# Eight sample rows ride along as extra columns of the last token tile, and the S5 state products alternate between the two column halves of the array

## The chip, the cores and the metric

The kernel runs on one core of a Trainium2 chip, as one program. The metric is the device time of an execution in microseconds (us), the median of several. Five engines work side by side: TensorE (PE), whose matmuls stream a moving operand past stationary weights, VectorE (DVE), ScalarE (ACT), GpSimd (POOL), and SyncE (SP), which here only issues transfers. Each takes its instructions in order and waits for semaphores that the others raise.

## The reference

One layer of a hybrid model is computed in fp32, for a prompt of 2048 tokens and for 8 sample rows (one new token of each of 8 sequences, with a carried S5 state):

```python
proj = x @ w_in                                   # 1024 -> 1536
u = gelu(proj[..., :512])
v = layer_norm(gelu(proj[..., 512:1024]), ln_v_g, ln_v_b)
xs = proj[..., 1024:]                             # 32 groups of 16
y_a = u * chunk_spatial_gate(v, w_s, b_s)         # chunks of 128 tokens; a sample row is a chunk of 1
y_b, h_re, h_im = s5_mixer(xs, h0, ...)           # a complex state of 64 numbers for each group
mix = concatenate([y_a, y_b]) @ w_out
x = layer_norm(ALPHA * x + mix, ln1_g, ln1_b)
x = layer_norm(ALPHA * x + grouped_moe(x, ...), ln2_g, ln2_b)
```

The outputs are the new rows of prompt and sample, the last S5 states of both, and the sample's normalised v.

## The kernel before

The work goes through stages, each a block of five engine programs with a barrier behind it. The change touches the first three.

**Precision.** Most products use operands split into a high and a low part (F32R), three matmuls for one: high x high, high x low, low x high (`PARTS`). The products of S5 are plain fp32, and one of these matmuls runs as two passes of weight load and matmul.

**Projection stage (to about 256 us).** Tokens go in 8 halves of 256 (`NH = 8`, `XH = 256`). PE transposes rows (`turn`, L690), ACT rounds them to the high part (`high`, L408), DVE takes the low part (`low`, L483); both parts lie in `xt[high/low][:, i % 2]`. `one(i, f, w)` (matmuls L702) forms 128 output channels x 256 tokens, 24 matmuls, for xs (`w = 0`, banks `pxs`, evicted by DVE at L496) and for u (`w = 1`, banks `pu`, evicted with the GELU by ACT at L420). From half 4 on PE also forms S5's matrices for one pair of groups after each tile (`pair_mats`, L720 and L729) from what DVE computes (`v_pair`, L637 to L640; `results`, L647, L649), while POOL computes another table (L377 to L380). ACT and DVE also split pieces of w_down, which SP loads and stores (L302, L295). In the last half the four xs tiles come first, with a `pair_mats` behind each, and then the four u tiles. Then ACT, DVE and POOL split the weights of v (L468, L674, L397), while PE runs 26 dummy matmuls, 52 passes (L789).

The 8 sample rows are transposed after the first half (`xts`, 8 columns for each k). Ahead of half 4 PE multiplies them on their own, with the sample as the stationary operand and 512 channels streamed past:

```python
for w, banks, out in ((0, pxs, xs_out), (1, pu, u_out)):
    pe.wait_ge(out, i * FT)
    for k in range(KD):
        for x, h in PARTS:
            mm = t.matmul(banks[0][0:NS, :], xts[x][:, k, :], (w_hi, w_lo)[h][w][:, k, :], ...)
    mm.then_inc(us_prod, 1)
pe.wait_ge(us_out, 2)
```

ACT (L455) and DVE (L654) evict the two results to `us[8, 2, 512]`, and SP stores the xs part (L313).

**Gate stage (to about 379 us).** PE forms v for 16 token tiles from the turned rows (L1138, `half` reloads them, L880), ACT applies the GELU, DVE normalises, PE multiplies by the chunk matrix (`gate`, L1116), DVE and POOL (L951, the last four tiles) multiply into u. The sample's v is one block of 24 matmuls (L1127), its gating is in `sample()` on DVE. SP spreads the stored xs of the sample into `us1`, with eight transfers of 4-byte pieces (L894).

**S5 stage (to about 470 us, then its gate).** There are 16 pairs of groups in quads of four. PE's order is `states(p + 1)`, `outputs(p)`, and so on, and after each quad 16 transposes (L1482) that wait for ACT (L1284, L1291). `states` multiplies 128 x 128 inputs by matrices for 64 state rows: group g = 0 goes to array columns 0 to 63, g = 1 to 64 to 127, with two accumulating 128-column matmuls (L1450) and one 8-column matmul for the sample (L1451) each, for the real and for the imaginary part. DVE scans (L1344 to L1366), and `outputs` has a part that needs no scan (L1461, L1462) and one that does (L1469). `load` (L815 to L817) brings a pair's inputs as soon as the outputs four pairs before are done. DVE's waits and the semaphores set the order; nothing is planned at run time.

Of the kernel before, what the change touches and what calls it, by code (L numbers as in the profile page):

```python
# [6 lines left out]
P = 128  # L7
F32 = mybir.dt.float32
# [7 lines left out]
ALU = mybir.AluOpType  # L16
# [81 lines left out]
def hybrid_step(nc, a, o):  # L98
    ctx = ExitStack()
    with ctx, nc.allow_non_contiguous_dma(reason="small parameters are laid out by state"):  # L100
# [28 lines left out]
        us_dram = dram("u_sample", [NS, WA])  # L129
# [5 lines left out]
        xt_dram = [dram(f"x_turned_{n}", [NH, P, KD * XH]) for n in ("high", "low")]  # L135
# [22 lines left out]
        xts = [sb(f"xts_{n}", [P, KD, NS], F32R) for n in ("high", "low")]  # L158
# [4 lines left out]
        us = sb("us", [NS, 2, WA])  # L163

# [8 lines left out]
        xt = [sb(f"xt_{n}", [P, 2, KD, XH], F32R, where=pa) for n in ("high", "low")]  # L173
        wv_raw = sb("w_v", [P, KD, WA], where=Place(nc, base))
        wv = [sb("wv_high", [P, KD, WA], F32R, where=Place(nc, base + 96 * KB)), sb("wv_low", [P, KD, WA], F32R, where=Place(nc, base))]
        pb = Place(nc, base + 96 * KB)
        xin = sb("xin", [P, 4, D], where=pb)
        xin_r = sb("xin_r", [P, 4, D], F32R, where=Place(nc, base + 96 * KB))
# [19 lines left out]
        with phase() as ph:  # L198
# [8 lines left out]
             dch, ach, gch, xsT_prod, xsT_out, k_stored, d_masked, kz, us_prod, us_out, cb_zero, k_zeroed, prm_row, prm_turned,  # L207
# [3 lines left out]
             cq_ready ust_ready dch ach gch xsT_prod xsT_out k_stored d_masked kz us_prod us_out cb_zero k_zeroed prm_row  # L211
# [42 lines left out]
            def _(sp):  # L254
# [51 lines left out]
                for i in range(NH):  # L306
                    if i < NH - 2:
                        sp.wait_ge(x_lo_set, 4 * i + 4)
                        for n in range(2):
                            sp.dma_start(xt_dram[n][i], xt[n][:, i % 2].bitcast(F32).rearrange("p k n -> p (k n)")).then_inc(xt_stored[i % 2], 16)  # L310
# [89 lines left out]
            def _(act):  # L400
                def high(c):
# [5 lines left out]
                    for h in range(2):  # L407
                        nc.scalar.copy(xt[0][:, i % 2, 4 * h:4 * h + 4, c % 2 * P:(c % 2 + 1) * P],  # L408
# [2348 lines left out]
```

## Time and profile before

| | us |
|---|---|
| median of 3 runs (lowest, highest) | 1299.25 (1299.21, 1302.53) |
| profiled execution, its own time | 1302.82 |
| its span in the trace | 1301.2 |
| PE busy in the span | 1213.3 (93%) |
| DVE, ACT, POOL busy | 901.8, 533.4, 483.9 |
| mean granted clock of PE | 0.972 |

The time of an execution is 1.6 us above its span. Busy time of PE counts overlapping matmuls as one stretch, and a matmul's end is modelled, so that start times tell more than durations. A granted clock of 1.00 is 2.4 GHz, and 0.50 is 1.2 GHz; a value between is a stretch with both.

### The profile page before, as it was taken

Reading aid. Unit: us, or ns where it says so; the run is one execution under the profiler, and the core shown is the slowest. Engines: PE = TensorE matmul, PEld = TensorE weight load, DVE = VectorE, ACT = ScalarE, POOL = GpSimd, SP = SyncE. Lnnn points to the kernel's source line nnn. Section 1 sums busy time; section 2 is a strip of 40 time slices with the busy share of each in tenths; the row PEclk is TensorE's granted clock in tenths of the full one; section 3 lists DMA queues with packets and bytes.
Section 4 is the critical chain, followed back from the end, with each engine's and each line's share of the span. In section 5 each row is a group of like instructions: output and inputs, shape, how many; then the busy total and the mean of one; then the engine's idle time right before and its main releaser. Section 6 shows DMA issues by size and latency. Waiting matters only on the chain. (4 is left out here: it accounts for less than half of the span.)

```text
span 1301.2 us, 24203 instructions
## 1 busy us (share of the span) xinstructions
PE 1213.3 (93%) x7245; PEld 1011.6 (78%) x7246; DVE 901.8 (69%) x1917; ACT 533.4 (41%) x881; POOL 483.9 (37%) x584
## 2 busy tenths in 40 slices
PE   7999999999878888999999688999999999999976
PEld 7997999978767755788887587888888888887852
DVE  3464886558868656557678567777787777777767
ACT  4131111111002346122333125666666666666656
POOL 3007880100031110623232033545555555455446
PEclk9999999999979989999999879999999999999988
DMA  8689593584436764246679565989889879756496
GB/s 246 192 316 290 181 267 123 170 265 167 160 106 211 216 223 120 100 155 240 236 265 300 200 259 210 293 266 322 262 270 327 257 230 294 196 155 169 107 296 254
DMA packets 141303, 290.08 MB, mean 223 GB/s; under 512 B 54634, under 2 KB 71610, under 8 KB 129940
## 3 DMA queue, kind: packets, MB, share of 16 engines
q1 hardware_dynamic: 122868, 225.70, 49.9%
q0 software_dynamic: 17328, 61.41, 19.2%
q10 hardware_dynamic: 1040, 2.10, 0.4%
q8 instruction: 39, 0.64, 0.2%
q14 instruction: 28, 0.23, 0.1%
HBM read 177.90 MB, written 111.13 MB: 222 GB/s over the span
## 5 line engine op out<-in xcount | busy, mean ns | idle before, releaser
L2407 DVE TENSOR_TENSOR wgu<-w_raw,wgu (+1 forms) x192 | 229.9, 1220 | 89.0 <-ACT wgu L2510 88.7
L2673 PE MATMUL p_gu<-wgu,xg_high 128*128 x768 | 244.4, 399 | 9.2 <-issue 4.6
L2510 ACT CAST wgu<-w_raw x188 | 192.7, 1052 | 62.2 <-issue 62.0
L2673 PEld LDWEIGHTS p_gu<-wgu,xg_high 128*128 128x128 f32 x768 | 139.7, 189 | 43.7 <-issue 17.3
L2673 PE MATMUL p_gu<-wgu,xg_low 128*128 x384 | 150.7, 392 | 0.0
L2272 POOL TENSOR_TENSOR spare_e<-nothing 128x1 f32<-128x1 f32 x48 | 46.5, 969 | 217.2 <-DVE yo L2426 217.2
L2273 POOL DMA_INDIRECT acc_rows<-yo,si x48 | 112.3, 2339 | 8.7 <-issue 8.5
L1995 PE MATMUL p_out<-w_out_high,mixt_high 128*128 128x512 f32 x256 | 102.3, 400 | 0.0
L1995 PE MATMUL p_out<-w_out_low,mixt_high 128*128 128x512 f32 x256 | 100.6, 393 | 0.0
L1995 PE MATMUL p_out<-w_out_high,mixt_low 128*128 128x512 f32 x256 | 100.6, 393 | 0.0
L2673 PEld LDWEIGHTS p_gu<-wgu,xg_low 128*128 128x128 f32 x384 | 72.1, 188 | 15.5
L2697 PE MATMUL p_d<-wd_high,ht_high 128*128 x192 | 80.2, 418 | 1.3 <-DVE ht_low L2420 1.3
L420 ACT ACTIVATE ya<-pu 128x256 f32<-128x256 f32 x32 | 12.2, 383 | 167.0 <-PE pu L702 167.0
L702 PE MATMUL pxs<-xt_high,w_xs_high 128*128 128x256 f32 x256 | 76.3, 298 | 2.7 <-DVE xt_low L483 2.0
L2697 PE MATMUL p_d<-wd_high,ht_low 128*128 x192 | 75.9, 395 | 0.0
L2697 PE MATMUL p_d<-wd_low,ht_high 128*128 x192 | 75.7, 394 | 0.0
L702 PE MATMUL pxs<-xt_high,w_xs_low 128*128 128x256 f32 x256 | 74.0, 289 | 0.0
L702 PE MATMUL pxs<-xt_low,w_xs_high 128*128 128x256 f32 x256 | 73.9, 289 | 0.0
L2400 DVE TENSOR_TENSOR xg_low<-p_xt,xg_high 128x512 fp32r<-128x512 f32 x96 | 61.8, 685 | 16.3 <-ACT xg_high L2497 16.1
L702 PE MATMUL pu<-xt_high,w_u_high 128*128 128x256 f32 x256 | 72.6, 284 | 0.0
L702 PE MATMUL pu<-xt_high,w_u_low 128*128 128x256 f32 x256 | 72.5, 283 | 0.0
L702 PE MATMUL pu<-xt_low,w_u_high 128*128 128x256 f32 x256 | 72.5, 283 | 0.0
(521 smaller groups left out, 2951.0 us busy)
## 6 DMA issues: line engine op xcount, KB each, us to landing
w_raw<-in_w_gate SPq DMA_DIRECT2D x16, 1024.0 KB, 7.3
w_raw<-in_w_up SPq DMA_DIRECT2D x16, 1024.0 KB, 9.9
wd_high<-w_down_high SPq DMA_DIRECT2D x16, 1024.0 KB, 6.7
wd_low<-w_down_low SPq DMA_DIRECT2D x16, 1024.0 KB, 9.0
ya_u<-in_w_down SPq DMA_DIRECT2D x38, 256.0 KB, 4.8
w_down_low<-ya_r SPq DMA_DIRECT2D x38, 256.0 KB, 5.7
acc_rows<-ax SPq DMA_DIRECT2D x18, 512.0 KB, 6.8
xin<-in_x_prompt SPq DMA_DIRECT2D x16, 512.0 KB, 5.3
```

The lines of the kernel that those rows point to most:

```text
L420: nc.scalar.activation(ya[:, 2 * i:2 * i + 2, f, :], pu[f % 2][:, 0:XH].rearrange("p (t n) -> p t n", n=P), ACT.Gelu_apprx_tanh).then_inc( ...
L702: mm = t.matmul(banks[f % 2][:, 0:XH], (w_hi, w_lo)[h][w][:, k, f * P:(f + 1) * P], xt[x][:, i % 2, k, :], start=(k == 0 and x + h == 0), ...
L1995: mm = t.matmul(po[b][m][0:n, :], mixt[x][:, b, k, 0:n], wo[w][:, k, m * SUP:(m + 1) * SUP], start=(k == 0 and x + w == 0), stop=(k == KD ...
L2272: gp.tensor_tensor(spare[:], nothing[:], nothing[:], ALU.add)
L2273: gp.indirect_dma_start(acc_dram, bass.IndirectOffsetOnAxis(ap=si[:, b:b + 1], axis=0), yo[:, b, :], None, compute_op=ALU.add).then_inc(ad ...
L2400: low = tt(xl[:, b, part, :], pt_x[h], xh[:, b, part, :].bitcast(F32), ALU.subtract)
L2407: low = tt(wgu[:, slot, 1, at], raw[:, slot, at], wgu[:, slot, 0, at].bitcast(F32), ALU.subtract)
L2510: nc.scalar.copy(wgu[:, slot, 0, at], raw[:, slot, at]).then_inc(hi_set, 1)
L2673: mm = t.matmul(pg[b][:, :, :], x[:, b, k, :], w[h][:, k], start=(k == 0 and x is xh and h == 0), stop=(k == KD - 1 and x is xl))
L2697: mm = t.matmul(pd[m][:, :], ht[x][:, b, k, :], w[h][:, k, m * SUP:(m + 1) * SUP], start=(k == 0 and x + h == 0), stop=(k == 1 and x == 1))
```

## The change

The sample rows become columns 256 to 263 of the odd buffer of turned rows, and the last half (7, odd) is projected 264 columns wide. Their results come out as [channel, sample] and are evicted by small extra instructions. In the gate stage the sample's u is multiplied after a transpose, and its xs is transposed back with four matmuls. In S5 the loops over h (which of the two accumulating matmuls) and g (which column half) are swapped, so that successive matmuls go to different halves.

```diff
-        xts = [sb(f"xts_{n}", [P, KD, NS], F32R) for n in ("high", "low")]
+        us_t = sb("us_t", [P, 2, FT, NS], where=Place(nc, us_at))
-        xt = [sb(f"xt_{n}", [P, 2, KD, XH], F32R, where=pa) for n in ("high", "low")]
+        XC = [XH, XH + NS]
+        xt = [[sb(f"xt_{n}{i}", [P, KD, XC[i]], F32R, where=pa) for i in range(2)] for n in ("high", "low")]
+        xts = [xt[n][1][:, :, XH:] for n in range(2)]
 # SP, projection
+                        if i % 2:
+                            sp.wait_ge(xsT_lo, 1)
-                    if i == NH // 2:
-                        sp.wait_ge(us_out, 2)
-                        sp.dma_start(us_dram, us[:, 1, :]).then_inc(k_stored, 16)
...
+                sp.wait_ge(xs_smp, FT)
+                sp.dma_start(us_dram.rearrange("(f p) n -> p f n", p=P), us_t[:, 1]).then_inc(k_stored, 16)
 # ACT, u_tile
+                    if i == NH - 1:
+                        nc.scalar.activation(us_t[:, 0, f, :], pu[f % 2][:, XH:XH + NS], ACT.Gelu_apprx_tanh).then_inc(u_smp, 1)
 # DVE, xs_tile
+                    if i == NH - 1:
+                        v.tensor_copy(us_t[:, 1, f, :], pxs[f % 2][:, XH:XH + NS]).then_inc(xs_smp, 1)
 # PE, one
+                    cols = XH + NS if i == NH - 1 else XH
+                    if i == NH - 1:
+                        pe.wait_ge(xsT_lo, 1)
+                        if f >= 2:
+                            pe.wait_ge((xs_smp, u_smp)[w], f - 1)
-                            mm = t.matmul(banks[f % 2][:, 0:XH], ..., xt[x][:, i % 2, k, :], ...)
+                            mm = t.matmul(banks[f % 2][:, 0:cols], ..., xt[x][i % 2][:, k, 0:cols], ...)
 # PE, ahead of half 4: the block of 48 matmuls quoted above, its waits and both evictions are gone
 # SP, gate stage
-                for n in range(NS):
-                    sp.dma_start(us1[P - Q:P, :, n], us_dram[n].rearrange("(g q) -> q g", q=Q)).then_inc(us_in, 16)
+                sp.dma_start(us1[P - Q:P], us_dram.rearrange("(g q) n -> q g n", q=Q)).then_inc(us_in, 16)
 # DVE, sample(): the 8x512 product is gone; at the end of the stage
-                v.tensor_copy(mixs_t[:, 0:FT, :], pmt[:, :].rearrange("p (f s) -> p f s", s=NS)).then_inc(mixa_set, 1)
+                v.tensor_tensor(mixs_t[:, 0:FT, :], pmt[:, :].rearrange("p (f s) -> p f s", s=NS), us_t[:, 0], ALU.mult).then_inc(mixa_set, 1)
+                v.tensor_copy(us[:, 1, :], psv[:, :]).then_inc(mixa_set, 1)
 # PE, after the last v tile
+                        for f in range(FT):
+                            mm = t.transpose(psv[:, f * P:(f + 1) * P], us_t[:, 1, f, :], ident[:])
 # PE, states
                     for r in range(2):
+                        lhs = [[smat[:, slot, h, r, g * N:(g + 1) * N] for h in range(2)] for g in range(2)]
+                        dst = [pst[b][g * N:(g + 1) * N, r, :] for g in range(2)]
+                        for h in range(2):
+                            for g in range(2):
+                                t.matmul(dst[g][:, 0:K], lhs[g][h], umat[:, slot, h, g, 0:K], start=(h == 0), stop=(h == 1))
                         for g in range(2):
-                            lhs = [smat[:, slot, h, r, g * N:(g + 1) * N] for h in range(2)]
-                            dst = pst[b][g * N:(g + 1) * N, r, :]
-                            for h in range(2):
-                                t.matmul(dst[:, 0:K], lhs[h], umat[:, slot, h, g, 0:K], start=(h == 0), stop=(h == 1))
-                            mm = t.matmul(dst[:, K:K + NS], lhs[1], umat[:, slot, 1, g, K:K + NS], start=True, stop=True)
+                            mm = t.matmul(dst[g][:, K:K + NS], lhs[g][1], umat[:, slot, 1, g, K:K + NS], start=True, stop=True)
```

Buffers behind the turned rows move by 512 bytes or 1 KB, and the stored turned rows get room for 264 columns a row block. These moves change no instruction count.

## Rows read from the trace of the kernel before

**Rows 1.** The windows of five stretches: busy us and instructions of each engine, clock, DMA.
```profile
114.80:126.80 12.00, 11.33 (x50) 4.19 (x49) 4.55 (x9) 0.97 (x2) 10.04 (x14) 1.00 0.94 268
159.00:164.00 5.00, 5.00 (x31) 5.00 (x31) 4.96 (x9) 0.00 (x0) 4.75 (x7) 0.66 0.69 218
256.50:367.00 110.50, 107.08 (x511) 87.03 (x512) 84.76 (x332) 11.42 (x20) 9.89 (x20) 0.98 0.53 180
371.00:386.00 15.00, 9.85 (x70) 9.51 (x71) 6.73 (x25) 0.00 (x0) 10.04 (x11) 0.54 0.54 158
390.00:470.00 80.00, 68.03 (x622) 55.47 (x618) 58.95 (x241) 28.66 (x54) 11.82 (x22) 1.00 0.63 198
```

**Rows 2.** The timeline of PE around the sample's block: start us, us, what.
```profile
114.74 0.28 PE L702 MATMUL pu<-xt_low,w_u_high 128*128 128x256 f32 x1
114.86 0.40 PE L772 MATMUL pxs<-w_xs_high,xts_high 128*8 128x512 f32 x1
...
126.81 0.39 PE L702 MATMUL pxs<-xt_high,w_xs_high 128*128 128x256 f32 x1 [0.67 <-ACT us L455]
```

**Rows 3.** The timeline of PE, first and last of one tile's 24 matmuls.
```profile
129.79 0.28 PE L702 MATMUL pu<-xt_high,w_u_high 128*128 128x256 f32 x1
...
132.55 0.28 PE L702 MATMUL pu<-xt_low,w_u_high 128*128 128x256 f32 x1
```

**Rows 4.** SP's timeline there, and the issues' view: KB, us to landing.
```profile
118.98 1.33 SPq L302 DMA_DIRECT2D ya_u<-in_w_down  x1
...
126.78 0.29 SPq L313 DMA_DIRECT2D u_sample<-us  x1
136.27 0.35 SPq L323 DMA_DIRECT2D sq_mats<-s_mat  x1
...
ya_u<-in_w_down SPq DMA_DIRECT2D x11, 256.0 KB, 5.1
```

**Rows 5.** The timeline in the last half, DVE and PE's weight loads.
```profile
233.65 0.22 DVE L649 COPY k_lag<-pkv 128x64 f32<-128x64 f32 x1
...
235.59 0.42 DVE L640 TENSOR_TENSOR v_im<-tv 128x256 f32<-128x256 f32 x1
236.31 0.14 PEld L720 LDWEIGHTS pst<-ident,v_re 128*128 128x128 f32 x1
...
237.06 0.68 DVE L647 COPY s_mat<-pst 128x512 f32<-128x512 f32 x1
...
238.94 0.07 DVE L671 MEMSET tm<- 128x16 f32 x1
```

**Rows 6.** The timeline at the end of the projection stage.
```profile
243.08 2.52 SPq L331 DMA_DIRECT2D k_lags<-k_lag  x2
...
247.78 5.35 DVE L674 TENSOR_TENSOR wv_low<-w_v,wv_high 128x512 fp32r<-128x512 f32 x4 [0.35 <-ACT wv_high L468]
...
249.26 5.96 PE L789 MATMUL tp<-ident 128*128 128x128 f32 x52
```

**Rows 7.** SP's timeline early in the gate stage.
```profile
258.20 1.35 SPq L887 DMA_DIRECT2D g_col<-in_ln_v_g  x1
```

**Rows 8.** The timeline at the end of the gate stage.
```profile
377.47 0.18 DVE L1105 COPY mixs_t<-pmt 128x32 f32<-128x32 f32 x1
...
377.64 1.26 POOL L951 TENSOR_TENSOR ya<-k_lag,ya 128x512 f32<-128x512 f32 x1 [0.44 <-DVE k_lag L1048]
```

**Rows 9.** The timeline of PE in two state products, at the low and full clock.
```profile
380.78 0.22 PE L1451 MATMUL p_state<-umat,sq 128*64 128x8 f32 x1
380.84 0.42 PE L1450 MATMUL p_state<-umat,sq 128*64 128x128 f32 x1
380.85 0.25 PE L1451 MATMUL p_state<-umat,sq 128*64 128x8 f32 x1
...
381.27 0.33 PE L1451 MATMUL p_state<-umat,sq 128*64 128x8 f32 x2
...
427.44 0.68 PE L1450 MATMUL p_state<-umat,sq 128*64 128x128 f32 x6
427.90 0.23 PE L1451 MATMUL p_state<-umat,sq 128*64 128x8 f32 x2
...
428.72 0.23 PE L1451 MATMUL p_state<-umat,sq 128*64 128x8 f32 x2
```

**Rows 10.** The waits of 380 to 470 us: total us, times, longest.
```profile
DVE rot L1344 <- PE p_state L1451: 10.9, 4, 3.2
```

**Rows 11.** The timeline of S5, DVE's hst and PE's outputs, and PE's wait.
```profile
399.41 0.28 DVE L1362 TENSOR_TENSOR hst<-rot 128x128 f32<-128x128 f32 x1
...
400.01 1.14 PE L1469 MATMUL p_y<-sq,hst 64*128 64x256 f32 x8
...
419.01 0.71 PE L1450 MATMUL p_state<-umat,sq 128*64 128x128 f32 x6 [1.47 <-DMA sq<-sq_mats]
```

More of the change, by code:

```diff
@@ L134, in hybrid_step @@
         NH = SEQ // XH
-        xt_dram = [dram(f"x_turned_{n}", [NH, P, KD * XH]) for n in ("high", "low")]
+        xt_dram = [dram(f"x_turned_{n}", [NH, P, KD * (XH + NS)]) for n in ("high", "low")]
         x1_dram = dram("x1_rows", [SEQ + NS, D])
@@ L407, in high @@
                     for h in range(2):
-                        nc.scalar.copy(xt[0][:, i % 2, 4 * h:4 * h + 4, c % 2 * P:(c % 2 + 1) * P],
+                        nc.scalar.copy(xt[0][i % 2][:, 4 * h:4 * h + 4, c % 2 * P:(c % 2 + 1) * P],
                                        tp[h][:, :].rearrange("p (k n) -> p k n", k=4)).then_inc(x_hi_set, 1)
@@ L443, in _ @@
                 act.wait_ge(xsT_prod, 1)
-                nc.scalar.copy(xts[0][:], tp[0][:, 0:KD * NS].rearrange("p (k n) -> p k n", n=NS)).then_inc(xsT_out, 1)
+                nc.scalar.copy(xts[0], tp[0][:, 0:KD * NS].rearrange("p (k n) -> p k n", n=NS)).then_inc(xsT_out, 1)
                 for f in range(FT):
@@ L452, in _ @@
                 for i in range(2, NH - 1):
-                    if i == NH // 2:
-                        act.wait_ge(us_prod, 2)
-                        nc.scalar.activation(us[:, 0, :], pu[0][0:NS, :], ACT.Gelu_apprx_tanh).then_inc(us_out, 1)
                     for f in range(FT):
@@ L480, in low @@
                     for h in range(2):
-                        part = (slice(None), i % 2, slice(4 * h, 4 * h + 4), slice(c % 2 * P, (c % 2 + 1) * P))
+                        part = (slice(None), slice(4 * h, 4 * h + 4), slice(c % 2 * P, (c % 2 + 1) * P))
                         dve.wait_ge(x_hi_set, 2 * c + h + 1)
-                        v.tensor_tensor(xt[1][part], tp[h][:, :].rearrange("p (k n) -> p k n", k=4),
-                                        xt[0][part].bitcast(F32), ALU.subtract).then_inc(x_lo_set, 1)
+                        v.tensor_tensor(xt[1][i % 2][part], tp[h][:, :].rearrange("p (k n) -> p k n", k=4),
+                                        xt[0][i % 2][part].bitcast(F32), ALU.subtract).then_inc(x_lo_set, 1)
                 def w_low(f):
@@ L699, in one @@
                         pe.wait_ge(out, n - 1)
+                    cols = XH + NS if i == NH - 1 else XH
[3 more added lines that the diff above has]
+                            pe.wait_ge((xs_smp, u_smp)[w], f - 1)
                     for k in range(KD):
                         for x, h in PARTS:
-                            mm = t.matmul(banks[f % 2][:, 0:XH], (w_hi, w_lo)[h][w][:, k, f * P:(f + 1) * P],
-                                          xt[x][:, i % 2, k, :], start=(k == 0 and x + h == 0), stop=(k == KD - 1 and x == 1))
+                            mm = t.matmul(banks[f % 2][:, 0:cols], (w_hi, w_lo)[h][w][:, k, f * P:(f + 1) * P],
+                                          xt[x][i % 2][:, k, 0:cols], start=(k == 0 and x + h == 0), stop=(k == KD - 1 and x == 1))
                     mm.then_inc(prod, 1)
@@ L766, in _ @@
                         pe.wait_ge(c_copied, 2)
-                        pe.wait_ge(xsT_lo, 1)
-                        for w, banks, out in ((0, pxs, xs_out), (1, pu, u_out)):
-                            pe.wait_ge(out, i * FT)
-                            for k in range(KD):
-                                for x, h in PARTS:
-                                    mm = t.matmul(banks[0][0:NS, :], xts[x][:, k, :], (w_hi, w_lo)[h][w][:, k, :],
-                                                  start=(k == 0 and x + h == 0), stop=(k == KD - 1 and x == 1))
-                            mm.then_inc(us_prod, 1)
-                        pe.wait_ge(us_out, 2)
                     for f in range(FT):
@@ L819, in hybrid_step @@
         with phase() as ph:
-            pt = Place(nc, base + 128 * KB)
+            pt = Place(nc, base + 129 * KB)
             wst = sb("wst", [P, HA, P], where=pt)
```

43 lines of the change are left out of this document (21 added, 22 removed).

## The prediction

> **What bounds the kernel now.** I read the windows by stage first [rows 1]. TensorE (PE) is busy for 11.33 of the 12.00 us around the sample's projection, and for 68.03 of the 80 us in the middle of the S5 stage. So time taken from PE is worth something where PE is the last to be ready, and nothing where it waits. Which of the two holds is read from the timeline, stage by stage. The change touches three stages: the input projection (to about 256 us), the spatial gate (to 379 us) and S5 (to about 470 us). Everything behind them (output projection, experts, last norm) keeps its instructions, and each of those stages starts behind a barrier, so it only moves.
>
> In the timeline of PE [rows 2] the reader should look at start times, not at durations. The ordinary matmuls before the sample start 0.12 us apart; the last one starts at 114.74. Then come the 48 matmuls of L772, and the first ordinary one afterwards starts at 126.81. The stretch is 11.95 us from 114.86 to 126.81, and there PE does nothing but the sample: 8 stationary columns with 512 streamed past, plus a last wait of 0.67 us for the GELU on ScalarE. In the steady run 24 such ordinary matmuls span 2.76 us from the first start to the last, 0.120 us each [rows 3].
>
> **Part 1, the sample leaves its own block.** Gone are the 48 matmuls, both waits for the evictions, the two evictions and PE's wait for them. Were the stretch cut out, the next matmul would start at 114.86. That is 11.95 us, all of it on PE. Is PE the last one there? VectorE (DVE) works 4.55 us of the 12, ScalarE (ACT) 0.97 [rows 1]. POOL is busy for 10.04 us, but with tables for S5 whose stores are due much later. So I take the full 11.95 us.
>
> What could be late next is SyncE's queue (SP). It issued a load of w_down at 118.98, whose kind lands 5.1 us after issue, and it then stood idle until the sample's result at 126.78, with the next transfer at 136.27 [rows 4]. After the change the first projection of the next half ends near 120.6, and ACT then wants to round that w_down piece, which is there only near 125.4 (118.98 + 1.33 + 5.1). ACT stands for about 4.5 us, and behind it in its queue is the rounding of the next turned rows. These are wanted by PE only at the next turn two projections later, some 14 us on, so I cost it at nothing. If that cover is gone it costs up to 4.5 us.
>
> **Part 2, 264 columns in the last half.** The last of the eight 256-row halves has 8 output tiles x 24 = 192 matmuls, each 8 columns wider. The trace has no width of 264. From below: nothing, if the start distance of 0.120 us is set by the weight load beside it. From above: in proportion to the columns, 0.120 x 8/256 = 3.75 ns, times 192 = 0.72 us. I take the middle, 0.35 us, since both are small. The Trainium skill (TensorE: Matmul & The Clock Gate, section Back-to-back issue gap) puts the distance at N/2.4 + 2.5 ns, 109 ns for 256 columns and 112.5 for 264. The measured 120 ns is above both; by the rule the sum would get 0.64 us here in place of 0.35.
>
> The small evictions: DVE copies 128x8 ahead of each of four xs tiles, ACT does a 128x8 GELU ahead of each of four u tiles. I bound one by a memset of 128x16, 0.07 us, and a copy of 128x64, 0.22 us [rows 5]. In the last half the loop PE -> DVE -> PE is close: DVE ends the second product of a pair at 236.01, PE starts to turn it at 236.31 [rows 5]. So there is 0.3 us of cover per tile against 0.07 to 0.22: nothing; without the cover 4 x 0.22 = 0.9 us. ACT's four are done while PE still spins: PE's dummy products run from 249.26 to 255.22, DVE is done at 253.13, ACT before that [rows 6].
>
> The store of the sample's xs goes from the middle to the end, as 512 pieces of 32 B, in SP's queue ahead of the two stores of k_lag. Its issue takes 0.29 us as the old one did [rows 4], or at most 1.35 us like the 512-piece load of g_col [rows 7]. The k_lag stores were issued by 245.6, and PE holds the barrier until 255.2 [rows 6]. Nothing. The odd halves of the turned rows are stored and reloaded 256 B per partition longer; no matmul of the gate stage waits for them, PE is busy for 107.08 of 110.50 us there [rows 1]. Nothing again.
>
> **Part 3, the gate stage.** One load instead of eight for the sample, of 32 B pieces instead of 4 B: SP's queue is some 3 us earlier, but nobody waits for it. Four extra transposes on PE stand ahead of the gates of the last tiles, which wait for DVE and POOL. At the end DVE multiplies 128x32 instead of copying it, and copies 8x512 more (0.18 us before [rows 8]; with the 0.68 us of a 128x512 copy [rows 5] it is 0.86, to 378.33), while POOL multiplies until 378.90 [rows 8]. Cover left: 0.5 us. DVE also loses one 8x512 product in the middle, where PE bounds. Nothing in all.
>
> **Part 4, S5's state products.** For a pair of groups PE runs 24 passes on a 64-column half each (an fp32 matmul is two passes). In the trace the first six 128-column passes start before the first 8-column pass [rows 9], although in program order the fourth is followed by two 8-column passes of the same half. And in the slow-clock stretch a 128-column pass (380.84) starts between two 8-column passes [rows 9]. So the chip already lets the other half overtake, once the first half's fourth weight load is out. From the first start 427.44 the 8-column passes start at 427.90 and then on to 428.72, 0.273 us for each of three more groups. Two groups, 0.55 us, are the time of one half; the second half merely starts one group late. Alternating should let it start at once: 0.27 us less a pair. With the clock low the same offset is 0.49 us, from 380.78 to 381.27 [rows 9]. From below the gain is nothing (the overlap is there already); from above all 16 pairs at 0.27 plus 0.2 us more at the low clock, 4.5 us.
>
> Where does it reach the end? The waits [rows 10] say that DVE waited 4 times for a state product, 10.9 us in all: at the first pair and at each quad's start, after the transposes. There a shorter product counts in full.
> - First pair, clock low [rows 9]: 0.5 us.
> - Rest of the first quad: the scans catch up. DVE ends hst at 399.69, the outputs start at 400.01 [rows 11]. Only 0.3 us can be gained.
> - Second and third quad: the first product counts (0.27, it also brings forward the load of the quad's last). The next two run into a wait for that load, 1.47 us at 419.01 [rows 11], and gain nothing. The last counts again. 2 x 2 x 0.27 = 1.1 us.
> - Last quad: DVE scans bound it after its first product: 0.27 us.
> Sum 2.2 us. The Trainium skill (TensorEngine Tiling, section Theoretical Speedup) promises up to 2x for a 64-wide operand. By it the products would halve, 1.3 to 0.65 us; the trace says that most of this is had already.
>
> **Sum.** -11.95 + 0.35 - 2.2 = -13.8 us. The profiled execution took 1302.82 us (its span 1301.2), 0.3% above the median of the runs, 1299.25; in its own terms it becomes 1289.0. From the median: 1285.5 us.
>
> **Rivals.**
> - *The order in S5 does nothing*, because the second half is held back by something else than the order (the issue of passes). For it: the groups run at an even 0.27 us. Against: with the clock at the lower level the offset grows to 0.49 us, so it is the array and not the issue. Then -11.95 + 0.35 = -11.6: 1287.6 us.
> - *The gap was SP's time to catch up.* The late w_down piece holds ACT 4.5 us and this reaches PE. For it: DMA share 0.94 in the gap [rows 1]. Against: the 14 us of cover above. -9.3: 1289.9 us.
> - *The halves run wholly side by side* (the rule of the second page above): the saving per counted product is 0.65 instead of 0.27, so 5 x 0.65 + 1.0 + 0.3 = 4.6: 1283.0 us.
> - *The clock falls in S5: slower than before.* With less work PE may no longer keep 2.4 GHz. Its granted clock was 1.00 in 390 to 470 at 85% busy, and 0.54 in 371 to 386 at 66% busy, after an idle stretch [rows 1]. At 1.2 GHz its 68 us of work would grow by up to as much again. It decides from about 16 us at the lower level (13.8/0.85); with half the stage it is +34 - 13.8 = +20: 1319 us. Against it: the change takes only 2 to 4 us of PE's 68.
> Beside these, single dips like 159 to 164 (clock 0.66) come or go with any shift, 1.7 us each way; they are part of each case's own range.
>
> **Chances.** Forecast 0.60 (1283 to 1288.5), no gain in S5 0.16, catching up 0.08, halves side by side 0.07, clock falls 0.05, and 0.04 for a gain eaten to within 0.3% by something not seen. A measurement of this kernel can tell about 0.3% from no change, 3.9 us. All cases but the last two lie beyond it: faster 0.91, same 0.04, slower 0.05. The range 1281.5 to 1291 takes in the first four cases with their dips.
>
> **What would show it.** In the new profile: no block of 128*8 matmuls in the projection, and PE's starts 0.12 us apart across the border of the halves; the last half's starts 0.120 to 0.124 apart; the projection's end 11.6 us earlier; the gate stage of the same length; the first and last 8-column passes of a pair's product 0.27 us nearer to the first start than 1.28; S5 shorter by 2.2 us, with the waits of DVE for p_state down by about 1.3. Wrong it would be if ACT or PE wait for DMA near the old gap, or PEclk in S5 drops.

## The result, and the profile after

The changed kernel took 1283.30 us (median of 4 runs, 1282.77 to 1285.56) against 1299.23 us for the kernel before beside it (4 runs): ratio 0.9876, 95% interval 0.9852 to 0.9900. That is 15.9 us less, between 13 and 19 by the interval. The forecast was 13.8 less, 1285.5 us. The profiled execution took 1283.07 us, its span 1281.4.

A comparison of two traces alone would mislead: the spans differ by 19.8 us. Some 3 us of that lie at the expert lists, whose code is the same, where the profiled execution before ran with TensorE (PE) at the lower clock. So I read each stage from its own first and last matmul, and over several kernels. Two kinds of stretch recur below: the projection, from the first turn of input rows to the last u matmul; and the gate stage's v stretch, from the first to the last v tile.

The windows of the kernel after, to be held against [rows 1]: length, busy us and count of PE, its weight loads, DVE, ACT, POOL, then granted clock, DMA share, GB/s.

```profile
114.80:126.80 12.00, 11.61 (x100) 11.37 (x99) 8.98 (x12) 2.36 (x5) 9.97 (x15) 1.00 0.98 315
250.00:360.50 110.50, 105.30 (x520) 85.23 (x519) 84.22 (x318) 12.03 (x21) 11.63 (x20) 1.00 0.49 177
371.00:386.00 15.00, 12.71 (x130) 10.46 (x127) 14.03 (x54) 2.48 (x7) 3.79 (x5) 0.97 0.68 200
390.00:450.00 60.00, 50.48 (x497) 40.96 (x496) 45.97 (x189) 20.87 (x39) 8.61 (x16) 1.00 0.66 204
```

In the first window 12 us hold 100 instructions on PE instead of 50: the block is gone and the ordinary projection stands there. DVE is busy for 8.98 us of it, not 4.55. S5 keeps its clock at 1.00.

PE's timeline at the border of the halves, where L772 stood before [rows 2], and one pair's product in S5, which answers to the full-clock rows of [rows 9]:

```profile
114.64 0.28 PE L709 MATMUL pu<-xt_low,w_u_high 128*128 128x256 f32 x1
114.76 0.28 PE L709 MATMUL pxs<-xt_high,w_xs_high 128*128 128x256 f32 x1
...
392.31 0.66 PE L1451 MATMUL p_state<-umat,sq 128*64 128x128 f32 x8
392.80 0.24 PE L1453 MATMUL p_state<-umat,sq 128*64 128x8 f32 x4
392.89 0.64 PE L1451 MATMUL p_state<-umat,sq 128*64 128x128 f32 x8
393.35 0.24 PE L1453 MATMUL p_state<-umat,sq 128*64 128x8 f32 x4
```

The border is 0.12 us wide. The product now runs as two even parts, and from first to last matmul it takes 1.08 us where it took 1.34 in all the kernels with the old order: 0.26 less, the forecast's 0.27. The first 8-column pass comes no earlier (0.49 us after the first start, 0.46 before [rows 9]); only the end does.

PE's waits in the projection stage (us, times, longest), first of the kernel before, then of the kernel after:

```profile
PE pxs L702 <- DVE xt_low L483: 2.0, 1, 2.0
PE pst L720 <- DVE v_im L640: 2.0, 1, 2.0
```

```profile
PE pst L727 <- DVE v_im L645: 4.3, 5, 1.4
PE pxs L709 <- DVE xt_low L486: 2.0, 1, 2.0
```

PE now waits five times for DVE's v_im, the second operand of the S5 matrices that PE turns between projections. The other traces agree: 3.4 to 4.3 us in three to five waits in the kernels with the change, 1.0 to 2.0 us in one wait in those before (e4 and e8, below, left aside).

PE's waits in the gate stage, before and after, the first of which the prediction had not looked at:

```profile
PE pg L1116 <- DVE ya L1058: 3.4, 1, 3.4
```

```profile
PE pg L1114 <- DVE ya L1057: 2.3, 1, 2.3
```

And what lay ahead of and behind the longer wait, first in the timeline of the kernel before:

```profile
342.98 0.68 DVE L1071 TENSOR_TENSOR mixs<-mixs,us 8x512 f32<-8x512 f32 x1
...
346.17 1.13 PE L1116 MATMUL pg<-wst,vn 128*128 128x128 f32 x8 [3.36 <-DVE ya L1058]
```

The windows behind it:

```profile
347.00:351.00 4.00, 4.00 (x13) 3.16 (x12) 3.19 (x12) 0.00 (x0) 0.55 (x1) 0.57 0.03 6
357.00:361.00 4.00, 4.00 (x21) 3.38 (x20) 3.23 (x12) 0.21 (x1) 0.55 (x1) 1.00 0.00 0
```

The product of the sample rows (L1071) is gone in the changed kernel. PE's wait is 1.1 us shorter, and the stretch with 13 instead of 21 matmuls in 4 us (granted clock 0.57, so mostly the lower of the two levels, 1.2 GHz) is gone too. The v stretch went from 110.17 to 108.19 us. The prediction had costed this edit at nothing.

S5's waits of DVE, the row of [rows 10] after the change; it is 2.2 us less, where the forecast was 1.3:

```profile
DVE rot L1345 <- PE p_state L1453: 8.7, 4, 2.3
```

### The profile page after: what moved, and what is told of

It is laid out like the page before. It is cut to its first block and busy times, and to the rows that moved or that the text cites. A ratio compares the mean times of both kernels' runs of the same rounds, so it can differ in the third digit from the quotient of the medians.

```text
span 1281.4 us, 24124 instructions
## 1 busy us (share of the span) xinstructions
PE 1193.0 (93%) x7201; PEld 997.3 (78%) x7202; DVE 908.0 (71%) x1920; ACT 533.6 (42%) x884; POOL 482.3 (38%) x584
## 3 DMA queue, kind: packets, MB, share of 16 engines
q0 software_dynamic: 17328, 61.41, 19.8%
## 5 line engine op out<-in xcount | busy, mean ns | idle before, releaser
L709 PE MATMUL pxs<-xt_high,w_xs_high 128*128 128x256 f32 (+1 forms) x256 | 75.4, 294 | 2.0 <-DVE xt_low L486 2.0
L709 PE MATMUL pxs<-xt_high,w_xs_low 128*128 128x256 f32 (+1 forms) x256 | 73.1, 286 | 0.0
L709 PE MATMUL pxs<-xt_low,w_xs_high 128*128 128x256 f32 (+1 forms) x256 | 72.9, 285 | 0.0
L1730 POOL TENSOR_TENSOR mixt_low<-ya,mixt_high 128x512 fp32r<-128x512 f32 x16 | 26.6, 1662 | 121.8 <-ACT mixt_high L1800 121.7
L709 PE MATMUL pu<-xt_high,w_u_high 128*128 128x256 f32 (+1 forms) x256 | 72.4, 283 | 0.0
L709 PE MATMUL pu<-xt_high,w_u_low 128*128 128x256 f32 (+1 forms) x256 | 72.2, 282 | 0.0
L709 PE MATMUL pu<-xt_low,w_u_high 128*128 128x256 f32 (+1 forms) x256 | 72.2, 282 | 0.0
```

The costliest lines, as they stand in the source:

```text
L709: mm = t.matmul(banks[f % 2][:, 0:cols], (w_hi, w_lo)[h][w][:, k, f * P:(f + 1) * P], xt[x][i % 2][:, k, 0:cols], start=(k == 0 and x + h ...
L1730: gp.tensor_tensor(mixt[1][:, b, part, 0:n], src, mixt[0][:, b, part, 0:n].bitcast(F32), ALU.subtract).then_inc(mix_low, 1)
```

## The experiments

Twelve kernels ran. Times are medians with the range; traces are of one execution each.

**The two halves of the change, and the kernel before again.** e0 is the kernel before, unchanged. e1 is the kernel before with the new order of S5's products alone (part 4; the diff), e2 is the kernel after with the old order.

```diff
-                            for h in range(2):
-                                t.matmul(dst[:, 0:K], lhs[h], umat[:, slot, h, g, 0:K], start=(h == 0), stop=(h == 1))
+                        for h in range(2):
+                            for g in range(2):
+                                t.matmul(dst[g][:, 0:K], lhs[g][h], umat[:, slot, h, g, 0:K], start=(h == 0), stop=(h == 1))
```

> The kernel before once more, for a second trace of it. Theory (the profiled execution of before was a slow one of its kind, because TensorE's clock was low during p_list): this execution takes about 1299.2 us, p_list takes 7.8 us instead of 10.7, and the dip of the clock near 160 us may be there or not. Rival (3.9 us of the 19.8 us between the two traces are the change's work behind S5): this trace shows the same 10.7 us for p_list as the first.

> The kernel before with the changed order of the S5 state products alone. Theory: a pair's product takes 1.08 us instead of 1.35 from its first weight load to the start of its last matmul; the last output of S5 comes 2.0 us earlier in the stage, as in the changed kernel, so 1297.0 to 1297.8 us, -1.5 to -2.2. Rival A (the order alone is worth nothing): within 0.3 us of 1299.2. Rival B (all sixteen products count): -4.5 us, 1294.7.

> The changed kernel with the S5 state products in their old order. Theory: -14 us against before, 1285.3 us, of which 12.0 in the removed block, and the rest is given back by TensorE's waits for v_im (4.3 us instead of 2.0) and gained by a dip of the clock that is absent. Rival (the recorded forecast, -11.6, nothing given back and no dip gained): 1287.6 us.

e0: 1302.09 us, one run. Its expert lists took 9.4 us, between the theory's 7.8 and the rival's 10.7, and its time was not lower: the theory did not hold, and the lists vary from run to run. e1: 1299.47 us (1295.08 to 1305.26), ratio 0.9991, interval 0.9973 to 1.0009. e2: 1285.17 us (1284.59 to 1288.11), ratio 0.9889, interval 0.9863 to 0.9914. So the columns carry almost all of the gain, and 2 us from the order alone cannot be told from nothing by its time; e2's interval holds both its theory's and its rival's time. Only e1's rival B, -4.5 us, is outside. The traces tell more. From the first state matmul to the end of the last outputs S5 takes, in the five kernels with the old order, 85.1 (before), 84.8, 84.6, 85.0 and 86.0 us; with the new order 83.3 (e1), 83.2 (after), 83.2 (e10) and 84.0 us (e3). That is 1.75 us between the medians, 85.0 and 83.25, against the 2.2 forecast. Two more with the new order had a fall of the clock in S5 or at its end and took 84.5 (e4) and 85.8 us (e11); counted in, they leave 1.3 us between the medians.

**264 columns in three halves instead of one (e3).**

```diff
-                    cols = XH + NS if i == NH - 1 else XH
+                    cols = XH + NS if i in (3, 5, 7) else XH
```

> The changed kernel with halves 3 and 5 projected 264 columns wide too; the 8 further columns are recomputed and thrown away. It has 384 more wide matmuls. Theory A (the width costs almost nothing, 0.02 us for a tile of 24, as half 7 showed): starts 0.120 to 0.121 us apart in half 5, and the whole at most 0.4 us longer. Theory B (cost in proportion to the columns, 3.75 ns each): 0.124 us apart and 1.4 us longer.

It took 1284.75 us in its one run, too near 1283.3 to tell the theories apart. What the width costs is read from the u tiles of 24 matmuls, first start to last. In halves 3 and 5 they take 2.78 us with 264 columns (e3) and 2.72 with 256 (after). But in the even halves, whose rows lie 256 columns apart, they take 2.76 us, as in the kernel before. So a tile of 264 columns costs 0.02 us more than a tile of the kernel before, over the last half's eight tiles 0.16 us, less than the 0.35 taken. And the new distance of 264 columns between the rows makes a 256-column matmul a little quicker, 0.118 against 0.120 us; 24 tiles in halves 1, 3 and 5 gain about 0.9 us. At one and the same distance, then, the 8 columns cost 0.06 us a tile, 2.6 ns a matmul and 0.5 us for the last half. The starts, 0.121 us apart, are as theory A said, but its reading that the width is almost free holds only together with that gain.

**Does GpSimd's load hold back DVE, and PE behind it? (e4 after, e8 before)** POOL builds one of the two S5 matrices (q_mat) with wide products beside DVE's. Here its products are cut to a sixteenth of their width; fifteen sixteenths of q_mat are zeros, so this part of the computation is left out. e8 is the same edit on the kernel before.

```diff
-    ch.mark(gp.tensor_tensor(t[k], x, y, ALU.mult))
+    ch.mark(gp.tensor_tensor(t[k][:, 0:1], x[:, 0:1], y[:, 0:1], ALU.mult))
...
-    gp.tensor_tensor(q_mat[:, b, 0], t[0], t[1], ALU.add).then_inc(q_ready, 1)
+    gp.tensor_tensor(q_mat[:, b, 0, 0:1], t[0][:, 0:1], t[1][:, 0:1], ALU.add).then_inc(q_ready, 1)
```

> The changed kernel with POOL's six products for S5's table (q_mat) in the projection stage cut to one 16th of their size; the table is mostly zeros and the outputs that rest on it are not the reference's. All instructions, waits and stores stay. Theory (DVE's operations are stretched up to 3 us while POOL's products run, and TensorE waits for v_im, 4.3 us in all): no DVE product of v_pair above 0.5 us, the wait for v_im at most 1 us, and the end of the projection 2 to 3.5 us earlier than 238.7 less 0.6 for a later start: 235 to 237 us. Rival (DVE is late because of its own work, without the pause that the sample's block gave it): the wait stays at 4 us and the end of the projection moves by less than 0.5 us.

> The kernel before with GpSimd's products for the state matrices cut to a sixteenth of their width (as in the run e4_pool_light on the kernel after); fifteen sixteenths of q_mat hold zeros, so this part of the computation is left out. It asks whether the projection gave back 1.5 us of the removed block because of this contention. Theory A (the contention costs the kernel before as much as the kernel after, about 3 us, and the block is worth 12.05 less 0.2 us of wider matmuls): the projection stage goes from 243.0 to about 241.3 us without a fall of the clock only where the contention mattered less before; that is, 229.44 + 11.85 = 241.3. Theory B (the contention costs both kernels the same, 3 us): about 240.0 us, and the missing 1.5 us lies elsewhere. The rest of the kernel as before.

e4: 1279.88 us (1276.72 to 1285.85), ratio to before 0.9871, interval 0.9843 to 0.9899. e8: 1298.02 us (1295.15 to 1301.86), ratio 0.9987, interval 0.9970 to 1.0004. The projection took 229.4 us in e4, and 231.7 to 233.5 in the full changed kernels without a fall of the clock; 241.6 us in e8, and 242.9 to 243.5 in the kernels before without one. So the contention costs the kernel after 2.3 to 4.0 us and the kernel before 1.3 to 1.9, each read against one trace with POOL quiet. The times don't resolve this: e4's ratio of 0.9871 is that of the kernel after (0.9876) within the noise. What happens behind the block is seen better from the start of half 4 to the last u matmul, since the part ahead of it differs by chance. It takes 120.2 to 120.5 us before (e0, e1, e9) and 122.9 to 123.9 after (after, e2, e6, e10); with POOL quiet 118.6 (e8) and 120.2 (e4). So some 3.2 us of the block come back, and with POOL quiet half of that, 1.6 us. The other half has another cause, shown below. DVE's groups show the mechanism; v_re is one product's result, 16 of them (total us, mean ns). First the kernel after, then e4:

```profile
L644 DVE TENSOR_TENSOR v_re<-tv 128x256 f32<-128x256 f32 x16 | 13.7, 855 | 0.6
L642 DVE TENSOR_TENSOR tv<-lv_im,bb_im 128x256 f32<-128x256 f32 x16 | 12.2, 763 | 0.0
```

```profile
L645 DVE TENSOR_TENSOR v_re<-tv 128x256 f32<-128x256 f32 x16 | 6.8, 425 | 0.5
L643 DVE TENSOR_TENSOR tv<-lv_im,bb_im 128x256 f32<-128x256 f32 x16 | 6.7, 420 | 0.0
```

The same instructions take 0.42 us each when POOL is quiet and 0.76 to 0.86 on average with its wide products there. One of the longest of the kernel after (the longest took 3.02 us) and PE's wait behind it:

```profile
141.93 2.99 DVE L642 TENSOR_TENSOR tv<-lv_im,bb_re 128x256 f32<-128x256 f32 x1
...
146.72 0.33 PE L727 MATMUL pst<-ident,v_re 128*128 128x128 f32 x1 [1.30 <-DVE v_im L645]
```

Of PE's waits for v_im e4 keeps a single one, 1.6 us in place of 4.3, and e8 none:

```profile
PE pst L728 <- DVE v_im L646: 1.6, 1, 1.6
```

e4's theory asked for at most 1 us. No DVE product of it is longer than 0.44 us, so this wait is not contention. Its timeline shows where it begins, at a load of w_down that ACT waits for:

```profile
123.88 0.62 ACT L431 CAST ya_r<-ya_u 128x512 fp32r<-128x512 f32 x1 [3.73 <-DMA ya_u<-in_w_down]
...
129.24 0.33 PE L728 MATMUL pst<-ident,v_re 128*128 128x128 f32 x1 [1.56 <-DVE v_im L646]
```

The same chain stands in the kernel after. PE had turned the next rows by 121.55 us. ACT stood before the w_down piece until 124.26 and only then rounded them; DVE, idle for 2.99 us, took their low part and worked without a pause until v_im was there at 130.11; PE waited for it (timeline):

```profile
124.26 0.62 ACT L430 CAST ya_r<-ya_u 128x512 fp32r<-128x512 f32 x1 [3.16 <-DMA ya_u<-in_w_down]
124.79 1.06 ACT L412 CAST xt_high<-tp 128x512 fp32r<-128x512 f32 x2
125.40 1.29 DVE L486 TENSOR_TENSOR xt_low<-tp,xt_high 128x512 fp32r<-128x512 f32 x2 [2.99 <-ACT xt_high L412]
...
129.69 0.42 DVE L645 TENSOR_TENSOR v_im<-tv 128x256 f32<-128x256 f32 x1
...
130.16 0.33 PE L727 MATMUL pst<-ident,v_re 128*128 128x128 f32 x1 [0.93 <-DVE v_im L645]
```

In the kernel before ACT found the piece there at the same step:

```profile
133.15 0.61 ACT L424 CAST ya_r<-ya_u 128x512 fp32r<-128x512 f32 x1
133.74 1.07 ACT L408 CAST xt_high<-tp 128x512 fp32r<-128x512 f32 x2
```

All nine kernels with the change have this wait of ACT, 2.4 to 3.7 us, and none of the five before. PE waits behind it in eight of the nine (0.8 to 0.9 us, 1.6 in e4). No run moved that load, so the chain is read from traces and not tested by an edit.

**Is S5 short of PE or of its loads? (e5, e6, e7)** e5 lets the 8 sample columns ride in the wide product, so that the eight passes of their own go. e6 lets ACT issue the loads of sq instead of SP. e7 has both.

```diff
-                             mm = t.matmul(dst[g][:, K:K + NS], lhs[g][1], umat[:, slot, 1, g, K:K + NS], start=True, stop=True)
+                             t.matmul(dst[g][:, 0:K + NS], lhs[g][1], umat[:, slot, 1, g, 0:K + NS], start=True, stop=False)
+                         for g in range(2):
+                             mm = t.matmul(dst[g][:, 0:K], lhs[g][0], umat[:, slot, 0, g, 0:K], start=False, stop=True)
...
-            sp.dma_start(sq[:, b], sq_dram[pair]).then_inc(pair_in[b], 16)
+                            act.dma_start(sq[:, b], sq_dram[i * 4 + 4 + b]).then_inc(pair_in[b], 16)
```

> The changed kernel, with S5's sample columns in the same matmul as the prompt's: the half of the input that holds the sample goes first with 136 columns and the other is added on 128. A pair has 16 passes instead of 24. Theory (a 64-column half takes weight load and matmul one behind the other, 0.109 us for a 128-column pass and 0.057 for an 8-column one): a product takes about 0.85 us instead of 1.08; the last output of S5 moves by 5 x 0.23 = 1.1 us at most, less where loads are waited for: 1282.2 to 1283.0. Rival (loads bound S5 by now, nine waits of 9.1 us in all): the product gets shorter, the stage does not, 1283.3 within 0.3.

> The changed kernel, with the load of S5's matrices (sq) issued by ACT's queue instead of SP's, whose five other issues for a pair take 4.1 us instead of 4.85. Theory (since the products are shorter, S5 is bound by SP's issue of loads, 4.85 us for a pair against 3.8 of TensorE's work): the waits for DMA fall from 9.1 us to less than 4, S5 ends 1 to 2 us earlier: 1281.5 to 1282.5. Rival (the waits are for the bytes, or DVE's scans bound anyway): waits or end of S5 unchanged, 1283.3 within 0.3.

> Both of the last two edits. Theory: the shorter product counts once the loads are early, 1280.5 to 1282 us, 1.3 to 2.8 less than the changed kernel's 1283.3. Rival: DVE's scans (4.1 us a pair) bound and nothing beyond the better of the two single edits is gained.

e5: 1286.44 us (1280.83 to 1289.92), ratio 0.9893, interval 0.9869 to 0.9916. e6: 1288.76 us (1283.0 to 1296.01), ratio 0.9927, interval 0.9899 to 0.9955. e7: 1291.43 us (1287.38 to 1295.4), ratio 0.9941, interval 0.9922 to 0.9961. None is faster than the kernel after. All three medians lie above their theories' times, though e5's interval still reaches its own; e7 gains nothing on either single edit, as its rival had it.

In e5 a product takes 0.85 us instead of 1.08, and yet S5 is as long as after, 83.2 us to the end of the outputs. One part of this is a stretch at the lower clock in e5's second and third quad (granted clock 0.58 from 406 to 410 us), from the sixth to the tenth pair's product 22.7 us against 21.3. The two other parts are without one: from the first product to the sixth pair's e5 is 0.74 us shorter, from the tenth pair's to the end 0.69. Five products, each 0.23 shorter, are 1.15 us in the first of these, and seven are 1.6 in the second. So 1.4 of 2.8 us arrive, about half of what PE saves; the rival (loads bound S5) holds for the other half only. What PE meets there is seen in the kernel after. SP issues the loads of a pair in 4.8 to 4.9 us (timeline of SP's queue):

```profile
401.60 3.07 SPq L813 DMA_DIRECT2D umat<-u_blocks  x4
404.83 0.67 SPq L814 DMA_DIRECT2D umat<-us  x1
405.69 0.45 SPq L815 DMA_DIRECT2D sq<-sq_mats  x1
406.44 3.07 SPq L813 DMA_DIRECT2D umat<-u_blocks  x4
```

and PE, which without a wait needs 3.8 us from one pair's product to the next, stands before the quad's last (timeline of PE):

```profile
426.22 0.66 PE L1451 MATMUL p_state<-umat,sq 128*64 128x128 f32 x8 [1.24 <-DMA sq<-sq_mats]
```

All such waits of PE, 366 to 456 us:

```profile
PE p_state L1451 <- DMA sq<-sq_mats: 3.6, 4, 1.2
```

Taking one of the six transfers of a pair away from SP did not help: in e6 the wait for sq fell, one for umat took its place, and S5 grew from 83.2 to 88.8 us (waits of e6, same stretch, the last row of SP's queue from 385 us):

```profile
PE p_state L1455 <- DMA umat<-us: 4.9, 3, 2.6
PE p_state L1455 <- DMA sq<-sq_mats: 1.4, 1, 1.4
...
SPq L813 <- PE p_y L1475: 12.3, 4, 4.2
```

SP itself waits 12.3 us in e6 for the outputs that free a slot, 2.0 in the kernel after. So its issue time is no longer what is short there, and my theory that less of it makes S5 faster was wrong. Why the umat loads come late in e6 was not found; part of its length is PE at the lower clock for 3.4 us from 428.4.

**The gate stage (e9, e10).** e9 is the kernel before without the 8x512 product L1071 and the wait ahead of it; the sample rows then lack their factor, so that part is left out (first two lines of the diff). e10 is the kernel after with the sample rows' work on DVE split in two and moved from behind the norm of tile 10 to behind those of tiles 13 and 14.

```diff
-                    ch.settle()
-                    v.tensor_tensor(mixs[:, 0, :], mixs[:, 0, :], us[:, 0, :], ALU.mult).then_inc(mixa_set, 1)
...
-            SMP = 10
+            SMP = 13
...
                     ch(normalise(vs[:], NS, 0, vs_var, vs_rstd, 1, vs[:]))
+                def sample_rest():
                     ch(v.tensor_tensor(vs[:], vs[:], gs_row, ALU.mult))
```

> The kernel before with the one 8x512 product of the sample rows on VectorE in the gate stage (L1071) and the wait ahead of it left out; the sample rows of mixs then lack their factor, so that part of the computation is left out. Theory A (this product makes the gate's wait 3.4 us instead of 2.3, and the longer wait lets the clock fall for 3.4 us): the stage from the first to the last v tile goes from 110.15 to 107.6 to 108.2 us, with no low clock in it and a wait for ya of about 2.3 us. Rival B (the shorter stage of the changed kernel comes from the buffers' or loads' new place): 110.1 us, low clock at about 346 us as before. The rest as before.

> The kernel after with the sample rows' work on VectorE in the gate stage moved from behind the norm of tile 10 (4.7 us in one piece) to behind those of tiles 13 and 14, where VectorE has about 2.4 us a tile left, half behind each. Theory A: the wait of the gate for ya (2.3 us in one place) goes, and nothing takes its place: the stage from the first to the last v tile goes from 108.17 to 105.9 us, the time from 1283.3 to about 1281.1 us, ratio to before 0.986. Rival B: VectorE is then late at the last three gate tiles, whose ya comes from GpSimd, and the 2.2 us show up between the last v and the last pg matmul (8.7 us now): no change in time.

e9: 1298.64 us, one run, against 1299.29 us for the kernel before on that chip. Its v stretch is 107.8 us and the wait 2.6 us, with no fall of the clock: theory A by the trace, and it names the step that the prediction missed. The time of one run can't show 2.4 us. e10: 1283.72 us (1279.91 to 1287.89), ratio 0.9885, interval 0.9862 to 0.9908, the same as the kernel after. Its v stretch is 105.7 us, 2.5 less, as theory A said, but from the last v matmul to the last pg matmul it takes 11.8 us instead of 8.5: rival B, the wait only moved. PE's timeline at the end of e10's stage:

```profile
351.31 1.05 PE L1118 MATMUL pg<-wst,vn 128*128 128x128 f32 x8
...
354.92 1.13 PE L1118 MATMUL pg<-wst,vn 128*128 128x128 f32 x8 [0.91 <-DVE ya L1057]
359.53 3.76 PE L1118 MATMUL pg<-wst,vn 128*128 128x128 f32 x16 [3.48 <-POOL ya L950]
```

DVE has no more than 0.67 us of idle time at a stretch (each the wait for POOL's root) from 330 us on in e10 and from 325 us on in the kernel after, until its last products for the gates. So the end of this stage follows DVE, wherever the sample's 4.7 us stand; only taking work off DVE shortens it, which is what the change did.

**Rows 272 columns apart (e11).** After the change, a v tile that reads its weights from an odd half's buffer takes 6.44 to 6.46 us instead of 6.37.

```diff
-        xt = [[sb(f"xt_{n}{i}", [P, KD, XC[i]], F32R, where=pa) for i in range(2)] for n in ("high", "low")]
+        XA = [XH, XH + 2 * NS]
+        xt = [[sb(f"xt_{n}{i}", [P, KD, XA[i]], F32R, where=pa) for i in range(2)] for n in ("high", "low")]
```

> The kernel after with the odd halves' rows of the turned x laid out 272 instead of 264 columns apart (1088 instead of 1056 bytes), the same columns used. Theory A (the v tiles of odd halves take 6.45 instead of 6.37 us because their weight rows begin at multiples of 32 but not of 64 bytes): at 272 they take 6.37 us like the even ones, and the stage from the first to the last v tile is 0.6 us shorter, 107.5 us. Rival B (any stride that isn't a power of two costs this, or the eight columns do): 6.45 us as now. The projection stage is as after in both, about 232.5 us without a fall of the clock.

It took 1286.52 us in one run. First matmuls of tiles 5, 6 (odd half from here) and 7, of the kernel after and of e11:

```profile
282.23 0.48 PE L1136 MATMUL pv<-wv_high,xt_high 128*128 128x512 f32 x1
288.60 0.48 PE L1136 MATMUL pv<-wv_high,xt_high 128*128 128x512 f32 x1
295.06 0.47 PE L1136 MATMUL pv<-wv_high,xt_high 128*128 128x512 f32 x1
```

```profile
282.81 0.48 PE L1137 MATMUL pv<-wv_high,xt_high 128*128 128x512 f32 x1
289.17 0.48 PE L1137 MATMUL pv<-wv_high,xt_high 128*128 128x512 f32 x1
295.63 0.48 PE L1137 MATMUL pv<-wv_high,xt_high 128*128 128x512 f32 x1
```

Tile 5 takes 6.37 and 6.36 us, tile 6 takes 6.46 in both. The theory that 64-byte multiples would help falls. This run also shows a wait and a clock that do not go by a simple bound:

```profile
335.76 1.13 PE L1115 MATMUL pg<-wst,vn 128*128 128x128 f32 x8 [2.36 <-DVE ya L1058]
```

The window behind it:

```profile
337.00:340.40 3.40, 3.40 (x10) 2.66 (x9) 2.63 (x9) 0.00 (x0) 0.55 (x1) 0.51 0.05 12
```

Its v stretch was 109.8 us, 1.6 more than after, for that one stretch at the lower clock. Such a stretch at this place came in all four kernels whose wait was 3.3 or 3.4 us (before, e0, e1, e8), in none with a wait of 0.9 (e10), and in one, this one, of nine whose wait was 2.2 to 2.6 us. The length of the wait doesn't settle it by itself: in the projection stage PE waits 1.3 to 1.5 us near 193 us in eight kernels, and a stretch at the lower clock begins there in four of them (e3, e5, e7, e11).

## Why the prediction was right, and where its sum was off

The direction, the size and the stage were right; 1283.3 lies in the range. The sum was -13.8 us, and the median moved by -15.9. That the sum comes this near is in part luck: it took 1.1 us too much for the projection and left out 2.3 us at the gate. Its terms, each against several traces:

- **The block, -11.95.** Right as a block. Against e0, the lead of the kernel after at the start of a projection pair rises by 12.0 us over the block. But the projection as a whole became only 10.5 us shorter, by the means: 242.9 to 243.5 us in three kernels before without a fall of the clock (e0, e1, e9), 231.7 to 233.4 in four after (after, e2, e6, e10). Followed pair by pair against e0, the lead is 0.6 us at the second pair (the first input rows), +0.8 from the quicker odd halves, +12.0 at the block, -3.75 at the waits for v_im, -0.2 in the last half: 9.4. The first of these is chance, since the same code takes 15.3 to 17.1 us there in the 14 traces. The step that was incomplete is "is PE the last one there?". PE was, but the 12 us had also served others: w_down's piece landed in them, and DVE got ahead in them, as the smaller cost of contention before suggests. Without them DVE is late at five places in the kernel after, at one behind that piece, and at the other four behind products that POOL stretched; e4, with POOL's products cut, has only the first.
- **264 columns, +0.35.** Measured 0.16 net, and that is the sum of two effects: at the new distance between the rows the 8 columns cost 2.6 ns a matmul, 0.5 us in all, and the distance itself gives most of it back. The rule of the Trainium skill (TensorE: Matmul & The Clock Gate, section Back-to-back issue gap), which the section gives for a matmul by itself and not for a stream with weight loads, makes the width 3.3 ns, 0.64 us. These traces are near it in the difference (118 to 121 ns) and not in the distances (109 and 112.5 by the rule). What was not foreseen is the stride's gain of 0.9 us in halves 1, 3 and 5, and its loss of 0.1 us in each v tile of the odd halves, about 0.7 us by the last.
- **Late w_down piece, nothing.** Wrong by about 1 us. ACT did wait for it, 3.2 us instead of the 4.5 worked out, which was among the recorded signs of being wrong, and PE waited 0.93 us behind it (the chain is above, under e4). The prediction looked at when PE wants the rounded rows, and there the cover of 14 us held. It did not look at DVE, which takes their low part first and makes v_im after it. As the rival *the gap was SP's time to catch up* had it, the late piece reaches PE, but with a fifth of the 4.5 us. Waits of ACT, 110 to 130 us:

```profile
ACT ya_r L430 <- DMA ya_u<-in_w_down: 3.2, 1, 3.2
```

- **Gate stage, nothing.** Wrong by 2.3 us. The prediction said that DVE loses a product "in the middle, where PE bounds". PE's total of 107.08 in 110.50 us [rows 1] hid a wait of 3.4 us at one gate. From the first v to the first state matmul the stage took 122.9 to 123.3 us in four kernels before and 120.9 in seven after (all but e10 and e11); e9 shows that the one product accounts for it: 120.7 us without it. In the v stretch 0.7 us of that is the wait itself, 1.6 the stretch at the lower clock.
- **S5's order, -2.2.** The product shrank by 0.26 us as forecast, and the stage by 2.0 (85.1 to 83.2 us to the end of the outputs); e0 and e1 give 1.4. The transposes behind it then ran at the lower clock in the kernel after (from 450.5 us, granted clock 0.50) and gave back 0.75, so that to the last transpose S5 was only 1.2 us shorter. That it isn't all of the 2.2 fits e5, where about half of a shorter product arrived; the forecast's count of the pairs in which it arrives was a little high. The rival *halves wholly side by side* is out (0.26 instead of 0.65 less), and *the order does nothing* too.
- **The clock falls in S5** did not come: 1.00 from 390 to 450. Single stretches of 3.4 us came in e5, e6 and e11, four in e7, and in e4 one began 1.2 us before the end of the outputs. The longest S5 among these was e7's, 91.2 us, and part of that is its waits: nothing near the +34 of the rival.

The terms measured from the traces add up to -10.5 - 2.3 - 1.75 us (S5 by the medians above), so -14.5, inside the interval of -13 to -19. The last 1.4 us of the median's 15.9 I can't assign. Behind S5 the code is the same, and yet from the first matmul of the output projection to the end of the span the traces take 786.8 to 791.5 us in the five kernels before and 782.3 to 789.7 in the nine with the change. It goes with where the clock falls: 35 to 44 us of it are at the lower level in the seven shortest, 41 to 50 in the seven longest. The list stage is one place (9.2 to 10.5 us in four of the five before, 7.5 in seven of the nine after, from its first to its last matmul). Whether the change has a part in this is not shown.

## What to carry to other kernels

When a block of work leaves the busiest engine, ask what the other engines and the loads in flight did meanwhile: here 12.0 us left and some 3 came back, about half with DVE's products that POOL stretches, about half with a load that had landed in that time. Follow a late load through every engine that stands behind it, not only to the one that bounds. A mean busy share of 97% does not say that the engine never waits; list its waits before costing an edit on another engine at nothing. And before shortening products in a pipelined stage, count in how many steps something else (a load, the engine behind) is as late: here 1.4 of the 2.8 us saved arrived.

## What the runs showed of the hardware

- A DVE product of 128x256 takes 0.42 us when POOL's products are narrow; in the kernel after, beside POOL's wide ones, it takes 0.54 to 0.86 on average, by its place in the sequence, and up to 3.02 us. Four of the delays reached PE there, with 0.2 to 1.4 us each.
- Two matmuls on different column halves overlap even when the order in the program is one half after the other; ordering them in turn takes a 24-pass product from 1.34 to 1.08 us, not to half.
- Rows 264 columns apart as the moving operand: 0.118 us from matmul to matmul of 256 columns instead of 0.120, and 0.121 for one of 264 columns. As the stationary operand of 512-column matmuls: 6.46 us a tile instead of 6.37, and the same at 272. No run here shows why.
- After a wait of 3.3 to 3.4 us PE ran a stretch at 1.2 GHz, four times of four; after 2.2 to 2.6 us once of nine. The price was 1.6 us, more than the 0.7 us by which the wait itself was longer. In another stage waits of 1.3 to 1.5 us were followed by such a stretch in four kernels of eight.
